# Neighbourhood attention: the softmax division moved from the probabilities to the values' product

## The reference, cut to what matters

```python
sc = jnp.einsum('bjqhd,bjkhd->bhjqk', qb, kg).astype(jnp.float32) * scale + bias
pr = jax.nn.softmax(sc, axis=-1).astype(vg.dtype)
o = jnp.einsum('bhjqk,bjkhd->bjqhd', pr, vg)
...
h = h + jnp.concatenate([oa, ob], axis=-1) @ w_out[i]
```

## Time and profile before

| | us |
|---|---|
| median of 3 runs (lowest, highest) | 1562.6 (1559.85, 1563.41) |
| profiled execution | 1559.29 |
| its span | 1557.3 |
| busy: TensorE, VectorE, ScalarE, POOL | 1517.0, 708.2, 528.3, 167.5 |
| TensorE's clock granted over the span | 0.999 |
| the loop i = 0 to 18, first to last product | 893 to 972 |

### The profile page before, as it was taken

The page is one execution under the profiler, slowest core; times in us unless marked ns, Lnnn a source line. Parts: engine busy times, 40 slices in busy tenths (PEclk is TensorE's granted clock), DMA queues, the critical chain, the costliest instruction groups (busy, mean ns, idle before and its releaser), DMA issues.

```text
span 1557.3 us, 19596 instructions
## 1 busy us (share of the span) xinstructions
PE 1517.0 (97%) x7812; PEld 1063.1 (68%) x7812; DVE 708.2 (45%) x1162; ACT 528.3 (34%) x907; POOL 167.5 (11%) x174
## 2 busy tenths in 40 slices
PE   6999999999999999999999989999999999999998
PEld 6776788888888888888877767754444444444366
DVE  5335332465444444468666788541122132132174
ACT  5234422354332423345355587421100011010042
POOL 1024100002111111110400210020000000000000
PEclk9999999999999999999999999999999999999999
DMA  8121422312222223222101132789999999999951
GB/s 332 45 72 62 189 94 95 122 66 87 105 108 90 100 82 108 108 95 82 54 30 53 68 150 76 307 342 391 421 420 421 421 421 421 420 422 420 421 231 55
DMA packets 45612, 311.73 MB, mean 200 GB/s; under 512 B 5184, under 2 KB 5696, under 8 KB 10192
## 3 DMA queue, kind: packets, MB, share of 16 engines
q1 hardware_dynamic: 42480, 296.74, 47.9%
q0 software_dynamic: 3040, 13.72, 2.4%
HBM read 302.05 MB, written 8.39 MB: 199 GB/s over the span
## 4 chain that ended last, share of the span: by engine, by line
PE 91%; DVE 4%; ACT 2%; issue 1%; DMA 1%; SPq 0%; DVEq 0%; ACTq 0%
PE bank L803 21%; PE bank L2532 14%; PE bank L2548 7%; PE bank L1465 7%; PE bank L838 7%; PE bank L855 4%; PE bank L2515 4%; PE bank L2565 4%; PE bank L2724 3%; PE bank L1322 3%; PE bank L816 2%; PE bank L826 2%; PE bank L873 1%; PE bank L847 1%; PE bank L864 1%
## 5 line engine op out<-in xcount | busy, mean ns | idle before, releaser
L627 DVE TENSOR_TENSOR w_lo<-M,w_hi 128x2048 fp32r<-128x2048 f32 x73 | 169.0, 2321 | 181.0 <-ACT w_hi L622 181.0
L2532 PE MATMUL bank<-M 128*64 128x512 f32 x1024 | 226.6, 595 | 1.0 <-ACT M L2620 1.0
L622 ACT ACTIVATE w_hi<-M 128x2048 fp32r<-128x2048 f32 x73 | 139.1, 1912 | 144.7 <-PE bank L803 56.9
L803 PE MATMUL bank<-HTL,w_hi 128*128 128x512 f32 x432 | 168.1, 389 | 0.0
L803 PE MATMUL bank<-HTH,w_lo 128*128 128x512 f32 x432 | 168.1, 389 | 0.0
L803 PE MATMUL bank<-HTH,w_hi 128*128 128x512 f32 x432 | 168.1, 389 | 0.0
L2532 PEld LDWEIGHTS bank<-M 128*64 128x64 f32 x1024 | 71.9, 137 | 134.7 <-issue 133.7
L2548 PE MATMUL bank<-M 128*64 128x512 f32 x512 | 113.6, 595 | 1.5 <-DMA M<-in_w 1.5
L2686 DVE TENSOR_TENSOR X<-bank,X 128x512 f32<-128x512 f32 x69 | 46.5, 688 | 109.7 <-PE bank L2565 109.6
L803 PEld LDWEIGHTS bank<-HTH,w_lo 128*128 128x128 f32 x432 | 81.1, 188 | 16.9
L803 PEld LDWEIGHTS bank<-HTH,w_hi 128*128 128x128 f32 x432 | 81.1, 188 | 16.8
(11 more groups left out here) (376 smaller groups left out, 2820.4 us busy)
## 6 DMA issues: line engine op xcount, KB each, us to landing
M<-in_w SPq DMA_DIRECT2D x192, 1024.0 KB, 11.2
M<-in_wd SPq DMA_DIRECT2D x78, 1024.0 KB, 4.8
M<-in_nb SPq DMA_DIRECT2D x4, 1536.0 KB, 7.3
X<-in_x SPq DMA_DIRECT2D x4, 512.0 KB, 7.4
M<-in_tb POOLq DMA_DIRECT2D x8, 256.0 KB, 4.6
M<-in_rows POOLq DMA_DIRECT2D x4, 512.0 KB, 6.5
rowb<-in_rows POOLq DMA_DIRECT2D x4, 512.0 KB, 6.1
xs_parts<-XSH POOLq DMA_DIRECT2D x1, 2048.0 KB, 10.4
```

The source lines that it names most:

```text
L622: e.activation(hi[:, :], slots[slot_of[n]], ACT.Copy).then_inc(split_hi_done, 1)
L627: e.tensor_tensor(lo[:, :], slots[slot_of[n]], hi[:, :], ALU.subtract).then_inc(split_lo_done, 1)
L803: m = e.matmul(out[:, :], w[:, k0 + k, n0:n0 + 128], v[k], start=(k == 0 and i == 0), stop=(k == len(hi) - 1 and i == 2))
L2532: m = e.matmul(b[64 * s:64 * s + 64, :], Xe[:, 4 * kh + k, o + C * s:o + C * s + C], unit_w(key, 4)[:, k, :], start=(kh == 0 and k == 0), ...
```

## The change

The exponentials are no longer multiplied by the reciprocal sums. They are transposed and multiplied with the values as they are. The reciprocals of a unit are spread by TensorE: for each head g a product has the reciprocals' column, repeated 32 times, as weights and the identity as moving operand, so that output rows 32g to 32g+31 hold the reciprocal of each query (`nbr_recip_pe`, bank `nr`, 7, one bank for a group's four blocks). After a group ScalarE copies that bank to SBUF (`N_RS`), VectorE multiplies the values' product by it into `N_NO` in token order, ScalarE copies the high part to `HTH` (`no_hi_act`, one step later), and VectorE subtracts for the low part (`no_lo_dve`). The transposes wait for `n_exp` instead of `n_norm`. The `no` banks become 6 alone, and the second transposes' bank of unit 1 goes from 7 to 4. `out2_pe` and `out2_pool` wait for `no_lo` instead of the banks.

```diff
--- before.py
+++ after.py
@@ -240,8 +240,8 @@
         h_sq, h_ms, h_sqrt, h_rope, h_qn = (sem(n) for n in ("h_sq", "h_ms", "h_sqrt", "h_rope", "h_qn"))
         gains_set, pl_sq, lam_dot, lam_exp = sem("gains_set"), sem("pl_sq"), sem("lam_dot"), sem("lam_exp")
         d_mx, d_w, d_pv = sem("d_mx"), sem("d_w"), sem("d_pv")
-        q_spread, n_exp, n_norm, n_pv, no_hi = (
-            sem(n) for n in ("q_spread", "n_exp", "n_norm", "n_pv", "no_hi"))
+        q_spread, n_exp, n_recip, n_pv, no_hi, no_lo = (
+            sem(n) for n in ("q_spread", "n_exp", "n_recip", "n_pv", "no_hi", "no_lo"))
         o_sq, o_ms, o_sqrt, o_norm, o_hi = (sem(n) for n in ("o_sq", "o_ms", "o_sqrt", "o_norm", "o_hi"))
         rt_sel, rt_pre, rt_wexp_in, rt_wexp, rt_w32, rt_done = (
             sem(n) for n in ("rt_sel", "rt_pre", "rt_wexp_in", "rt_wexp", "rt_w32", "rt_done"))
@@ -390,7 +390,7 @@
                 O2A_PARTS.setdefault(i, []).append((n % 4, n // 4, low))
             O2A_SUM[steps[1]] = (n % 4, n // 4)
         nt_turn = itertools.cycle((0, 5, 3))
-        NBR_BANKS = {"vj": (4, 0, 3, 6, 4, 0, 5, 3), "oa": {2: 7, 3: 4}, "ns": (1, 2), "nt": ((0, 5), (3, 7)),
+        NBR_BANKS = {"vj": (4, 0, 3, 6, 4, 0, 5, 3), "oa": {2: 7, 3: 4}, "ns": (1, 2), "nt": ((0, 5), (3, 4)),
                      "o2a": (4, 4, 4, 4, 4, 1, 2, 4)}
         for i in range(len(NBR) + 3):
             if 0 < i < len(NBR):
@@ -404,7 +404,8 @@
                 if not low:
                     ps.put(("o2a", t, h), [NBR_BANKS["o2a"][t + 4 * h]])
             if i >= 3 and (i - 3) % 4 == 0:
-                ps.put(("no", (i - 3) // 4), [6 + (i - 3) // 4 % 2], counted=False)
+                ps.put(("no", (i - 3) // 4), [6], counted=False)
+                ps.put(("nr", (i - 3) // 4), [7])
             if 2 <= i <= len(NBR) + 1:
                 for half in range(2):
                     ps.put(("nt", i - 2, half), [NBR_BANKS["nt"][i - 2][half] if i < 4 else next(nt_turn)])
@@ -2033,7 +2034,6 @@
         N_PT = [spare[:, 0:D].rearrange("p (a b) -> p a b", a=8), region(10240, 8, 128)]
         NBR_ST = [[stat(4) for _ in range(3)] for _ in NBR]
         k4 = kbT.rearrange("p f (r c) -> p f r c", c=64)
-        catR = [v[:, :, :].rearrange("p f (r c) -> p f r c", c=64) for v in (HTH, HTL)]
 
         def nbr_sp(e):
             taken(e, ("do", 3))
@@ -2065,6 +2065,17 @@
                                  k4[half, hg, :, KB[j]:KB[j] + 32], start=True, stop=True)
                     if s:
                         m.then_inc(fills, 1)
+
+        def nbr_recip_pe(e, i):
+            hg, j = NBR[i]
+            rr = NBR_ST[i][2]
+            b, fills = claim(e, ("nr", hg)) if j == 0 else (held(("nr", hg))[0], fills_of(("nr", hg)))
+            e.wait_ge(n_recip, i + 1)
+            for g in range(4):
+                m = e.matmul(b[32 * g:32 * g + 32, j * 128:(j + 1) * 128], rr[:, g:g + 1].to_broadcast([128, 32]), ident,
+                             start=True, stop=True, tile_position=(0, 32 * g))
+            if j == 3:
+                m.then_inc(fills, 1)
 
         def nbr_pe(e):
             for i in range(len(NBR) + 3):
@@ -2090,8 +2101,10 @@
                                 taken(e, ("oa", f))
                         high_ready(e, ("out2", 2 * h))
                         gemm_rows_part(e, ("out2", 2 * h), t, claim(e, ("o2a", t, h))[0], 0)
+                if i >= 3:
+                    nbr_recip_pe(e, i - 3)
                 if 2 <= i <= len(NBR) + 1:
-                    e.wait_ge(n_norm, i - 1)
+                    e.wait_ge(n_exp, 4 * (i - 1))
                     for half in range(2):
                         b, fills = claim(e, ("nt", i - 2, half))
                         for g in range(4):
@@ -2126,6 +2139,16 @@
                 e.activation(N_P[i % 3][:, g, :], N_SC[i % 2][:, g, :], ACT.Exp, scale=-1.0, bias=nm[:, g:g + 1],
                              accum_out=rs[:, g:g + 1]).then_inc(n_exp, 1)
 
+        N_RS, N_NO = region(14912, 512), region(15424, 512)
+
+        def no_hi_act(e, hg):
+            taken(e, ("no", hg))
+            e.activation(HTH[:, 4 + hg, :], N_NO, ACT.Copy).then_inc(no_hi, 1)
+
+        def no_lo_dve(e, hg):
+            e.wait_ge(no_hi, hg + 1)
+            e.tensor_tensor(HTL[:, 4 + hg, :], N_NO, HTH[:, 4 + hg, :], ALU.subtract).then_inc(no_lo, 1)
+
         def nbr_act(e):
             taken(e, ("do", 3))
             for i in range(len(NBR) + 3):
@@ -2135,14 +2158,10 @@
                     oa_hi_act(e, OA_AT[i])
                 for v in VJ_ACT.get(i, ()):
                     evac_act(e, Vj[:, v, :], ("vj", v))
+                if i >= 4 and NBR[i - 4][1] == 3:
+                    no_hi_act(e, NBR[i - 4][0])
                 if i >= 3 and NBR[i - 3][1] == 3:
-                    hg = NBR[i - 3][0]
-                    e.wait_ge(n_pv, i - 2)
-                    for jj in range(4):
-                        b, _ = held(("no", hg))
-                        e.activation(catR[0][:, 4 + hg, :, 16 * jj:16 * jj + 16],
-                                     b[:, jj * 128:(jj + 1) * 128].rearrange("p (r c) -> p r c", c=16),
-                                     ACT.Copy).then_inc(no_hi, 1)
+                    evac_act(e, N_RS, ("nr", NBR[i - 3][0]))
                 if 2 <= i <= len(NBR) + 1:
                     j = i - 2
                     if j >= 2:
@@ -2159,6 +2178,7 @@
                     if i == 16:
                         e.wait_ge(q_spread, 16)
                     split_act(e, unit["out2", O2_SPLIT[i]])
+            no_hi_act(e, 3)
 
         def nbr_score_dve(e, i):
             hg, j = NBR[i]
@@ -2184,11 +2204,10 @@
                     oa_lo_dve(e, OA_AT[0])
                 if 1 <= i <= len(NBR):
                     nm, rs, rr = NBR_ST[i - 1]
-                    P = N_P[(i - 1) % 3]
                     e.wait_ge(n_exp, 4 * i)
-                    dve_own.mark(e.reciprocal(rr, rs))
-                    e.wait_ge(dve_own.sem, dve_own.n)
-                    e.tensor_tensor(P, P, rr.unsqueeze(2).to_broadcast([128, 4, 256]), ALU.mult).then_inc(n_norm, 1)
+                    e.reciprocal(rr, rs).then_inc(n_recip, 1)
+                if i >= 4 and NBR[i - 4][1] == 3:
+                    no_lo_dve(e, NBR[i - 4][0])
                 if i == 2:
                     oa_lo_dve(e, OA_AT[2])
                 if i - 1 in O2_SPLIT:
@@ -2197,22 +2216,21 @@
                     out2_add(e, "o2a", *O2A_SUM[i])
                 if i >= 3 and NBR[i - 3][1] == 3:
                     hg = NBR[i - 3][0]
-                    e.wait_ge(no_hi, 4 * hg + 4)
-                    for jj in range(4):
-                        b, empties = held(("no", hg))
-                        hi, lo = (v[:, 4 + hg, :, 16 * jj:16 * jj + 16] for v in catR)
-                        o = e.tensor_tensor(lo, b[:, jj * 128:(jj + 1) * 128].rearrange("p (r c) -> p r c", c=16), hi,
-                                            ALU.subtract)
-                    o.then_inc(empties, 1)
+                    taken(e, ("nr", hg))
+                    e.wait_ge(n_pv, i - 2)
+                    by_row = lambda v: v.rearrange("p (j r c) -> p j r c", j=4, c=16)
+                    b, empties = held(("no", hg))
+                    e.tensor_tensor(N_NO.rearrange("p (r j c) -> p j r c", j=4, c=16), by_row(b[:, :]), by_row(N_RS),
+                                    ALU.mult).then_inc(empties, 1)
+            no_lo_dve(e, 3)
 
 
         def out2_pe(e):
-            for hg in range(3):
-                taken(e, ("no", hg))
+            e.wait_ge(no_lo, 3)
             for h in range(2):
                 split_ready(e, ("out2", 2 * h + 1))
                 gemm3_rows(e, ("out2", 2 * h + 1), 4, 0, claim(e, ("o2", 0, h))[0], range(3))
-            taken(e, ("no", 3))
+            e.wait_ge(no_lo, 4)
             for t in range(TT):
                 for h in range(2):
                     b, fills = claim(e, ("o2", t, h)) if t else (bank[ps.at["o2", 0, h][0]], fills_of(("o2", 0, h)))
```

## The result

The changed kernel takes 1567.32 us, median of 7 runs (1565.97 to 1570.37), against 1561.21 us of the kernel before in the same runs (7 runs, 1559.85 to 1563.41): a ratio of 1.0043, 95% interval 1.0034 to 1.0053. Forecast were +5.2 us.

The account below looks back on a forecast made before the run. TensorE, busy 97% of the span, was taken as the bound. Insertions of 7.1 us less 1.1 absorbed early and 0.8 later gave +5.2, added to the 1562.6 us median: 1567.8 us, range 1562.5 to 1570.5.

Parts of the forecast that it names:

- The bound: Whole kernel: TensorE busy 97% of the span; in the changed stage VectorE holds it early and later hardly at all.
- An insertion: A step's four new products before its transposes: 0.48 us in twelve steps, 0.36 in three, 0.22 in step 18; gross 7.1.
- the rule on the change of shape: Changing tiling mode drains TensorE: with it the insertions sum to 7.1 us, without it to 3.5.
- Absorbed early: Up to the scores of step 5: insertions of steps 3 and 4 (0.84 us) absorbed and 0.25 won, 1.1 us.
- From there TensorE runs on: From step 4's scores at 910.7, 5.05 us of TensorE work without waits; step 5's scores at 915.75, before 916.00.
- the bank 4 claim of the transposes: Early steps: the transposes' second half claims bank 4, left by VectorE's L1925, which can start at 908.4, not 908.81.
- Absorbed later: From step 5 on, remaining TensorE idle before scores and before step 6's high halves closes: 0.8 us.
- the wait of 1.0 us for the sum: Steps 7 and 8: TensorE still waits 1.0 us for L2241, now because VectorE's low-half subtraction waits for ScalarE's high half.
- the single banks of products and sums: Banks 6 and 7: free at 925.8 and 924.6, claimed by TensorE only at 928.6 and 927.6.
- the low half at the end: Stage end: product, multiply, high and low half take about 2.3 us, behind 4.1 us of TensorE's L873 products.
- VectorE has over 1 us before its result gates anything of TensorE: Behind the stage: POOL's gain load is issued about 0.6 us later, with over 1 us of slack on VectorE.
- The total: Whole kernel: +5.2 us, 1567.8 us by the median, 1564.5 for the profiled execution.

Follow-up runs that it names:

- third: The kernel of the first experiment with the spreading products moved behind the transposes, right before the value products; ratio 1.0009 to the kernel before.
- fifth experiment: The kernel of the first experiment with every spreading product made twice in a row in the same place; ratio 1.0047 to the kernel before.
- first experiment: The changed kernel with unit 1's second transposes in bank 0 instead of 4 and later transposes' banks in the order 5, 3, 0; 1565.2 us, ratio 1.0023.
- second: The kernel before with only unit 1's second transposes moved from bank 7 to bank 4; ratio 1.0004.
- seventh experiment: The kernel before with VectorE adding the projection's tile to X before a step's reciprocals and multiply, up to step 15; ratio 0.9996.
- fourth: The kernel of the first experiment with spreading products for a group's last block only, 4 of 16 insertions; ratio 0.9999 to the kernel before.
- sixth experiment: The changed kernel with spreading products beside the value products, VectorE's sum first, and early ScalarE order and banks mended; 1559.4 us, ratio 0.9993 to the kernel before.

## Why the prediction was right, and where it was off

- **The bound.** TensorE in the stage, and VectorE only early: right. VectorE lost 17.7 us of work (forecast about 19) and the kernel got slower.
- **An insertion.** 0.48, 0.36 and 0.22 us forecast, 0.50, 0.36 and 0.24 measured. Worked out from differences of starts around L2112 it held to 0.02 us, and the rule on the change of shape decided between 3.5 and 7.1 us; the third and the fifth experiment show it.
- **Absorbed early.** This step failed in part: "From there TensorE runs on". The freed bank 7, the bank 4 claim of the transposes and the start of step 4 at 910.7 were right. I followed the moved transposes to who leaves bank 4 to them, and not to who takes it after them. That was the 2.4 us; without it (first experiment) the scores of step 5 start at 915.70 and the stage is 5.21 us longer, against 915.75 and 5.2, and the last value products at 976.72, forecast 976.8.
- **Absorbed later.** 0.8 forecast, 1.0 measured; the wait of 1.0 us for the sum kept its size with a new cause, as forecast.
- **The rest.** Neither the single banks of products and sums nor the low half at the end held TensorE: from the last value products to the first L874 it went on without idle time (979.16 to 979.71), and there is no wait at L874. But "VectorE has over 1 us before its result gates anything of TensorE", on POOL's gain load, failed. These are VectorE and TensorE behind the stage, first before, then after:

```profile
983.55 1.29 DVE L700 SCALAR_TENSOR_TENSOR M<-X,st,M 128x1024 f32<-128x1024 f32 x1 [1.87 <-DMA M<-in_rows]
996.46 1.09 PE L732 MATMUL bank<-cst,M 128*128 128x128 f32 x8 [0.46 <-DVE M L700]
...
992.84 1.28 DVE L701 SCALAR_TENSOR_TENSOR M<-X,st,M 128x1024 f32<-128x1024 f32 x1 [3.59 <-DMA M<-in_rows]
1004.62 1.09 PE L733 MATMUL bank<-cst,M 128*128 128x128 f32 x8 [1.07 <-DVE M L701]
```

  VectorE already waited for that load before; now it waits 1.7 us longer, 0.6 of them from the later issue as forecast and the rest from a longer transfer (10.0 us instead of 8.9), and TensorE waits 0.6 us more. Its next wait is 0.3 shorter (1.38 instead of 1.64), so 0.3 us are lost up to there; in the first experiment, with a transfer of 9.5 us, nothing is.
- **The total.** +7.64 us in the stage where 5.2 were forecast, the 2.4 between them; +6.1 by the medians. That the time itself, 1567.3 us, comes so near the 1567.8 forecast is luck: the 5.2 were added to a median of three runs, 1562.6, which with seven runs is 1561.2, and the 2.4 us that were overlooked fill that gap and more.

## What to carry to other kernels

Where TensorE is the bound, work taken off another engine is paid for by every product added, and a small product in another tile shape costs its way in and out as well: put it next to work of its shape, here half the price. When a buffer is moved, follow the new bank both ways: who leaves it, and who claims it next in every engine's order. And look for the stretch in which the relieved engine holds the bound one: the change taken there alone, with the order of work mended, gave the only kernel here whose interval lies below 1. When a change and a mend go in together, run the mend alone too: here one of the mends by itself was worth 1.1 us of a stage.

## What the runs showed of the hardware

- Eight fp32 products of 32 output rows each start in fours; a group of four more costs 0.11 us (0.23 us for two, fifth experiment).
- TensorE's granted clock fell to the lower level for a few us in some profiles and not in another with the same work: 0.58 and 0.57 from 911 to 915 us in the second and seventh experiment, after six us in which TensorE was busy 3.60. The kernel before was busy 3.60 of the same six as well (903.53 to 909.53 there, as its stage starts earlier), and the clock stayed at 1.00. What decides between them no run here shows. It made eight instructions of scores last 2.08 us instead of 1.14, and the way to step 5 0.80 us longer. No profile of a kernel with the moved division shows it in this stage.
- The mean granted clock of an execution goes with its time. Of 59 executions of the kernel before that were measured beside the experiments, three had 0.999, as its profiled one, and took 1559.0 us on average, 27 had 0.997 and took 1561.1, and eleven had 0.996 and took 1562.2. The kernels of the third, fourth and sixth experiment had 0.998 or 0.999 in all of theirs. The sixth is 1.2 us faster by the medians with a stage that is 0.2 longer, which fits that: its five executions at 0.998 take 1560.4 us on average, against 1559.7 of the eight such ones of the kernel before. Whether the moved division keeps the clock up, or something else does, is not shown.
